# Layer 2: the first two products of the output projection start inside the attention

## The reference

```
def odd_mixer(h_lat, h_ctx, w_in, w_out, sink, cos, sin, ctx_out):
    q, k, v = odd_project(h_lat, w_in)
    ...
    y, yc = window_gqa_sink(q, k, v, qc, kc, vc, sink, ctx_out)
    return y @ w_out, ((yc @ w_out) if ctx_out else None)
...
        x_lat = layer_norm(DN_ALPHA * x_lat + m_lat[2] * y_lat, ln_g[l, 0], ln_b[l, 0])
        f_lat = conv_ffn(modulate(x_lat, m_lat[3], m_lat[4]), ffn_w_up[l], ffn_conv_w[l], ffn_conv_b[l], ffn_w_down[l])
        x_lat = layer_norm(DN_ALPHA * x_lat + m_lat[5] * f_lat, ln_g[l, 1], ln_b[l, 1])
```

## Time and profile before

| | |
|---|---|
| median of 3 runs | 2373.16 us |
| the profiled execution's own time | 2374.36 us |
| its span, first to last instruction | 2372.6 us |
| PE busy | 2282.4 us (96%) |
| DVE busy | 1564.1 us (66%) |
| ACT busy | 934.2 us (39%) |
| mean granted TensorE clock | 0.990 |

### The profile page before, as it was taken

How to read it: one execution, slowest core, us unless ns; L and a number is a source line. 1 busy time by engine, 2 the same in 40 slices (tenths; PEclk the granted TensorE clock), 3 DMA queues, 4 the chain that set the end, 5 groups by cost and what they waited for, 6 DMA issues and landing times.

```text
span 2372.6 us, 34992 instructions
## 1 busy us (share of the span) xinstructions
PE 2282.4 (96%) x14058; PEld 1868.4 (79%) x14058; DVE 1564.1 (66%) x2497; ACT 934.2 (39%) x1768; POOL 352.7 (15%) x455
## 2 busy tenths in 40 slices
PE   7999999999999899899999999999999999999998
PEld 3876667888887788777888888888887778888886
DVE  4548786566767652577779975656474877765457
ACT  5336553422222421576342332232352774424333
POOL 0110100011022210101010413213112120101131
PEclk9999999999999899999999999999999999999999
DMA  7430124644534312111322333324122112432321
GB/s 270 138 108 11 36 90 172 249 160 160 179 132 165 104 60 82 70 64 51 129 86 94 119 124 125 106 90 142 45 80 80 38 63 99 160 107 89 107 89 71
DMA packets 79473, 257.70 MB, mean 109 GB/s; under 512 B 5712, under 2 KB 10832, under 8 KB 70864
## 3 DMA queue, kind: packets, MB, share of 16 engines
q1 hardware_dynamic: 65888, 207.84, 25.4%
q0 software_dynamic: 12704, 46.14, 5.6%
q10 hardware_dynamic: 720, 1.47, 0.2%
HBM read 246.00 MB, written 9.44 MB: 108 GB/s over the span
## 4 chain that ended last, share of the span: by engine, by line
PE 48%; DVE 4%; ACT 2%; issue 1%; POOL 0%; POOLq 0%; DVEq 0%; ACTq 0%
PE PS L1310 8%; PE PS L1311 8%; PE PS L1312 8%; PE PS L1381 4%; PE PS L1382 4%; PE PS L1383 4%; PE PS L1182 1%; PE PS L1223 1%; PE PS L1279 1%; PE PS L1282 1%; PE PS L1280 1%; PE PS L1201 1%; PE PS L1016 1%; PE PS L1013 1%; PE PS L1014 1%
## 5 line engine op out<-in xcount | busy, mean ns | idle before, releaser
L1310 PE MATMUL PS<-HH,WH 128*128 128x512 f32 (+1 forms) x1088 | 420.4, 386 | 3.1 <-DVE WL L2401 1.7
L1311 PE MATMUL PS<-HL,WH 128*128 128x512 f32 (+1 forms) x1088 | 416.7, 383 | 0.0
L1312 PE MATMUL PS<-HH,WL 128*128 128x512 f32 (+1 forms) x1088 | 416.7, 383 | 0.0
L2811 ACT ACTIVATE WH<-STG 128x1024 fp32r<-128x1024 f32 (+1 forms) x202 | 196.9, 1023 | 270.1 <-PE PS L1383 222.2
L2401 DVE TENSOR_TENSOR WL<-STG,WH 128x1024 fp32r<-128x1024 f32 (+1 forms) x202 | 243.1, 1244 | 37.5 <-ACT WH L2811 37.3
L1923 DVE SCALAR_TENSOR_TENSOR ACC<-ADAW,CS,ACC 128x1024 f32<-128x1024 f32 x168 | 227.2, 1386 | 23.5 <-PE PS L1016 14.4
L1310 PEld LDWEIGHTS PS<-HH,WH 128*128 128x128 f32 x1088 | 204.4, 188 | 47.7 <-issue 6.2
L1312 PEld LDWEIGHTS PS<-HH,WL 128*128 128x128 f32 x1088 | 204.4, 188 | 40.4
L1311 PEld LDWEIGHTS PS<-HL,WH 128*128 128x128 f32 x1088 | 204.5, 188 | 40.0 <-issue 1.0
L1381 PE MATMUL PS<-WH,AH 128*128 128x512 f32 x600 | 234.9, 392 | 0.3 <-DVE AL L2629 0.3
L1382 PE MATMUL PS<-WL,AH 128*128 128x512 f32 x600 | 233.6, 389 | 0.0
(11 more groups left out here) (276 smaller groups left out, 4420.0 us busy)
## 6 DMA issues: line engine op xcount, KB each, us to landing
STG<-in_w_up SPq DMA_DIRECT2D x66, 1024.0 KB, 6.2
ADAW<-in_w_ada SPq DMA_DIRECT2D x96, 512.0 KB, 4.0
STG<-in_w_down SPq DMA_DIRECT2D x20, 1024.0 KB, 5.3
ADAW<-in_w_ada POOLq DMA_DIRECT2D x32, 512.0 KB, 4.1
STG<-in_w_ffn_out SPq DMA_DIRECT2D x10, 1024.0 KB, 7.3
STG<-in_ev_w_in SPq DMA_DIRECT2D x8, 1024.0 KB, 5.1
STG<-in_w_in SPq DMA_DIRECT2D x6, 1024.0 KB, 7.3
spill<-X POOLq DMA_DIRECT2D x10, 512.0 KB, 5.1
```

What stands on the lines that cost most here:

```text
L1310: e.matmul(out, h_, hh, start=c == 0, stop=False)
L1311: e.matmul(out, h_, hl, start=False, stop=False)
L1312: return e.matmul(out, l_, hh, start=False, stop=c == 7)
L2811: return e.activation(dst, src, ACT.Copy)
```

## The change

Only layer 2 is changed. Product (3,0) no longer stands in w_out: its first four chunks stand on PE behind the turning in turn 31 of the attention, its last four behind that in turn 32. Product (2,0) stands right behind the result of item 31, ahead of PE's wait for the other engines' ends. The other six products keep their order. So that this is possible, ACT makes the high parts of tile 3 in turn 30 and of tile 2 in turn 32, DVE the low parts of tile 3 in turn 31 and of tile 2 in turn 32; w_out keeps those of tile 4. The high part of tile 3 gets another place in REG, since at its old one lies the table of the window. The banks of the first two products are exchanged.

```
+def out_early(L):
+    return 2 if L == 2 else 0
@@ PE, woven_pairs
             if 1 <= i <= N:
                 turn(i - 1, 0)
+            if L == 2 and i in (N - 1, N):
+                out_product(2, 1, 0, range(4) if i < N else range(4, 8))
@@ PE, w_out
+        if L == 2:
+            out_product(2, 0, 0)
         for x in (k.dv_end, k.ac_end, k.pl_end):
             w.wait_ge(*x(("att", L)))
-        for i, n in out_order(L):
+        for i, n in out_order(L)[out_early(L):]:
+            out_product(L, i, n)
@@ PE, out_product (the loop body of before, in a function)
+        for c in cs:
+            wh, wl = k.out_weights(L, n, c // 4)
+            x = slice(c * P, (c + 1) * P)
+            w.wait_ge(*k.ac_xh((L, tt, c // 4)))
+            w.wait_ge(*k.dv_wolo((L, n, c // 4, c % 4 // 2)))
+            e.matmul(PS[:, b, :], xh[:, x], wh[:, c % 4, :], start=c == 0, stop=False)
+            e.matmul(PS[:, b, :], xh[:, x], wl[:, c % 4, :], start=False, stop=False)
+            w.wait_ge(*k.dv_xl((L, tt, c // 4)))
+            m = e.matmul(PS[:, b, :], xl[:, x], wh[:, c % 4, :], start=False, stop=c == 7)
@@ DVE, woven_pairs
                 inverse(i - 1)
+            if L == 2 and i == N - 1:
+                out_low(2, 1)
             if i >= 2:
                 result(i - 2)
             if 1 <= i <= N:
                 turned_p(i - 1, 0)
+            if L == 2 and i == N:
+                out_low(2, 0)
@@ ACT, woven_pairs
                 turned_p(i - 1, 0)
+            if L == 2 and i == N:
+                out_high(2, 0)
             if i < N:
                 powers(i, 1)
                 if L == 2:
                     sink(i)
+            if L == 2 and i == N - 2:
+                out_high(2, 1)
@@ DVE and ACT, w_out
-        for i in range(3):
-            low(i)
+        for i in range(out_early(L), 3):
+            out_low(L, i)
```

More of the change, by code:

```diff
@@ L370, in out_parts @@
         tt = WOUT_TT[L][i]
-        o = (10240, 11264, 0)[out_place(i)]
+        o = (10240, 12544 if L == 2 else 11264, 0)[out_place(i)]
         return self.split_att[L]["REG"][:, o:o + 1024], self.XL[:, tt * 1024:(tt + 1) * 1024]
@@ L1265, in pairs, with out_product @@
         a.close()
+    def out_product(L, i, n, cs=range(8)):
+        tt = WOUT_TT[L][i]
+        xh, xl = k.out_parts(L, i)
+        b = k.bank[("wo", L, tt, n)] if cs[0] else take(("wo", L, tt, n))
+        for c in cs:
[7 more added lines that the diff above has]
+            m = e.matmul(PS[:, b, :], xl[:, x], wh[:, c % 4, :], start=False, stop=c == 7)
+        if cs[-1] == 7:
+            m.then_inc(*k.pe_wout.up((L, tt) if n else (L, tt, 0)))
+            freed[b] = [k.dv_yg(("wo", L, tt, n))]
     def w_out(L, bg):
+        if L == 2:
+            out_product(2, 0, 0)
         for x in (k.dv_end, k.ac_end, k.pl_end):
             w.wait_ge(*x(("att", L)))
-        for i, n in out_order(L):
[L1271 to L1284, removed]
+        for i, n in out_order(L)[out_early(L):]:
+            out_product(L, i, n)
             if n:
@@ L1581, in tensor_program @@
         project(L)
-        rot["set"], rot["n"] = [6, 7], 0
+        rot["set"], rot["n"] = list(range(8)), 0
         scores_ready(L)
         woven_pairs(L, items_of(k, L))
-        rot["set"], rot["n"] = list(range(8)), 0
         e.drain().then_inc(*k.pe_end.up(("att", L)))
@@ L2237, in out_weights_low, with out_low @@
                         ALU.subtract).then_inc(*k.dv_wolo.up((L, n, h, i)))
+    def out_low(L, i):
+        xh, xl = k.out_parts(L, i)
+        tt = WOUT_TT[L][i]
+        for h in range(2):
+            x = slice(h * 512, h * 512 + 512)
+            w.wait_ge(*k.ac_xh((L, tt, h)))
+            e.tensor_tensor(xl[:, x], k.x(tt)[:, x], xh[:, x].bitcast(F32), ALU.subtract).then_inc(*k.dv_xl.up((L, tt, h)))
     def pairs(name, L, bg):
@@ L2410, in after @@
                 layer_norm("a", L, tt, [k.dv_x(("wo", L, tt, 1))])
[L2412 to L2418, removed]
         def regain(i):
@@ L2473, in w_out @@
             for x in out_made(L)[i]:
-                low(x)
+                out_low(L, x)
             if L and i != last - 1:
@@ L3032, in pairs, with out_high @@
         result(p)
+    def out_high(L, i):
+        xh, _ = k.out_parts(L, i)
+        tt = WOUT_TT[L][i]
+        if L == 2 and i < 2:
+            w.wait_ge(*k.dv_out((2, len(items_of(k, 2)) - 4 + (i + 1) % 2)))
+        if i >= 3:
+            w.wait_ge(*k.pe_wout((L, WOUT_TT[L][out_place_before(i)])))
+        for h in range(2):
+            x = slice(h * 512, h * 512 + 512)
+            copy(xh[:, x], k.x(tt)[:, x]).then_inc(*k.ac_xh.up((L, tt, h)))
     def woven_pairs(L):
@@ L3142, in norm @@
                 layer_norm("a", L, tt)
[L3144 to L3151, removed]
         for s in k.ends(("att", L)):
             w.wait_ge(*s)
-        for i in range(3):
-            high(i)
+        for i in range(out_early(L), 3):
+            out_high(L, i)
         for h in range(2):
@@ L3161, in w_out @@
             for x in out_made(L)[i]:
-                high(x)
+                out_high(L, x)
             if i == last:
```

## The result

The changed kernel takes 2378.61 us (median of 10 runs, 2377.67 to 2381.26), the kernel before in the same comparison 2373.14 us: +5.5 us, ratio 1.0023 with an interval of 1.0015 to 1.0031. The forecast was 2379.0. The profiled execution took 2378.48 us over a span of 2376.7.

The account below looks back on a forecast made before the run. PE bounds the feed-forward part, but a level chain of POOL's residual loads and DVE's work sets its start: 3.68 (later attention end) + 3.82 (SP's traffic) - 0.99 - 0.66 = +5.85 us, median 2379.0, range 2374.6 to 2380.8.

Parts of the forecast that it names:

- SP's fetch later: Feed-forward weight fetch, waiting for DVE's second piece of weights, goes from 1952.12 to 1953.55, only 1.43 us later.
- regain of tile 3 later: On DVE behind the residual loads: starts at 1968.1 instead of 1960.61, 7.5 us later; lower bound 3.68.
- DVE's waits for PE that go: DVE's waits of 0.99 and 0.66 us for PE's products vanish, since the products are done long before.
- The end of the attention: Two half products on PE, 2.72 us each, partly covering idle time, end the attention 3.68 us later; bounds 3.4 to 4.06.
- The early parts: ACT's and DVE's four early copies each hide in idle time and cost nothing; without that cover 0.5 us.
- PE's wait for weights: In w_out, PE needs the weights' second half at 1953.7 and gets it at 1952.4: no wait.
- The overtaking: SP's traffic keeps 3.4 us behind its issue and passes before tile 3 lands: 3.82 us more; forecast's chance 0.53.
- From the regain to the end: DVE's chain up to the second turn_mid: regain's 7.5 us less 1.65 of waits for PE gives 5.85 us later.
- The lost clock: Clock falls in PE's wait at turn_mid; 1.84 us lost in (5,0), covered to 0.2 us by 1.68 of later waits.
- No overtaking: Rival at the DMA queues: SP's traffic enters behind the same amount of POOL's; +2.0, 2375.2; chance 0.22.
- PE's gain: Rival at turn_mid: PE's 4.99 us come through if the POOL and DVE chain has room; 2368.3, chance 0.06.
- "worse" case: Rival: low clock pushes (5,1) and the first feed-forward product beyond DVE's chain; 2 to 3 us more, 2381.5; chance 0.05.

Follow-up runs that it names:

- e4: Changed kernel with product (3,0) in one piece behind the last result, ahead of (2,0), nothing inside the attention on PE: 2375.38 us, +2.6 against the kernel before.
- e1: Changed kernel with only (3,0)'s halves kept; product (2,0) and the parts of tile 2 back in w_out: 2376.93 us, +4.1 against the kernel before.
- e2: Changed kernel with only product (2,0) behind the last result; product (3,0) and tile 3's parts back in w_out: 2373.55 us, +0.7 against the kernel before.
- e3: Changed kernel with SP's first fetch of feed-forward weights held until tile 3's residual has landed: 2375.39 us, +2.6 against the kernel before.
- e6: Kernel before, with only SP's fetch held until tile 3's residual has landed: 2373.08 us, ratio 0.9998.
- e5: Edits of e2 and e3 together, one product behind the last result and SP's fetch held: 2370.63 us, -3.1 against the kernel before.
- e7: Kernel of e5 with POOL's two layer-norm gain loads issued behind the four residual tiles: 2370.70 us, -3.0 against the kernel before.
- e8: Changed kernel with SP's fetch held and the two gains loaded behind the residual tiles: 2371.06 us, -2.7 against the kernel before.

## Why the prediction was right

| step | predicted | measured |
|---|---|---|
| attention ends later | 3.68 | 4.17 |
| SP's fetch later | 1.43 | 1.94 |
| PE done with the products of tiles 2 to 4 earlier | 5.2 | 4.5 |
| more of SP's traffic ahead of tile 3 | 3.82 | 3.47 |
| regain of tile 3 later | 7.5 | 7.64 |
| DVE's waits for PE that go | 1.65 | both gone |
| second turn_mid later | 5.85 | 6.07 |
| time | +5.85 | +5.5 |

*The end of the attention.* The mechanism held, the term was 0.5 us too small, beyond the upper bound of 4.06 that I gave. The third matmul did not wait; what I left out are the borders between transposes and large matmuls: the row at 1942.39 is followed by the next matmul 0.34 us later and the last one, at 1945.02, by the inverse 0.32 us later, where I had 0.23, at four such borders, and a half starts 0.64 us behind its transposes, where I had 0.55. e4 against the changed kernel shows that the halves do it.

*The early parts.* I put them at nothing. In the changed kernel they are hidden; e4 shows 0.93 us where the half product doesn't cover them. I had put that price at 0.5.

*PE's wait for weights.* None, as predicted.

*The overtaking.* The mechanism held, the time came out so near by luck in part. I took SP's traffic to keep its 3.4 us behind the issue, with 1.88 MB of POOL's moved by then, 3.54 MB needed, and all of SP's 3.15 MB gone by before tile 3 lands, in either reading of the queues. None of this was exact. SP's first packet came 4.2 us behind the issue and its traffic in earnest 4.6 us, with 2.15 MB of POOL's moved; tile 3 needed 3.66 MB; POOL's queue had 0.159 MB/us beside SP's and not 0.145; and only 2.52 of SP's 3.15 MB had gone by. The later start and the higher need cost what the larger amount moved and the better rate give back, so the regain came at +7.64 against 7.5. The 3.82 us of the sum hide this: 1.11 MB more of SP's at 0.285 MB/us are 3.9 us, and 3.47 were measured.

Does SP's traffic start a fixed time behind its issue, or behind a fixed amount of POOL's? Five traces bear on it. Its first packet came 3.4 to 3.5 us behind the issue before, 4.2 in the changed kernel, 3.9 in e1 and e2, 4.2 in e4, with 2.8, 2.0, 2.3, 2.5 and 2.2 MB of POOL's moved in all. That speaks against the fixed 2.8 MB of the rival. Between issue and first packet POOL's moved 1.2 to 1.4 MB in all five; why SP's traffic waits so long stays open.

POOL's queue alone was slower than I thought, 0.25 MB/us from 1952 to 1955 against the 0.41 of the earlier trace rows, though all engines were busy; e3 shows that this stretch of its loads is slow without SP's traffic too (0.29). That the overtaking costs is shown by e3 (4.28 us less distance), by e6 (the regain 1.58 us earlier) and by the difference of e2 and e5 (2.5 us).

*From the regain to the end.* This step of the sum, the regain's shift less DVE's two waits for PE, is the best proved. In the changed kernel and in all eight experiments the distance is the shift of tile 3's regain, plus what DVE then waits for PE at the two places, less 1.65, within 0.16 us: 7.64 - 1.65 = 5.99 against 6.07 here, 3.39 - 1.65 = 1.74 against 1.79 in e3, -5.10 + 3.52 - 1.65 = -3.23 against -3.22 in e7.

*The lost clock.* As predicted, it costs nothing at the end: from (5,0) to the second turn_mid PE takes 18.78 us, 18.92 before, and its wait there fell from 1.31 to 0.16 us. The terms were off: the wait of 0.37 us ahead of the first feed-forward matmul stayed, so there was room for 1.31 us and not 1.68, and from (5,0) to that matmul PE lost 1.0 us (12.52 against 11.52) and not 1.84. A loss of 1.84 us would have gone 0.5 us beyond the room. The prediction names a rule by which transposes don't raise the clock, and the traces speak against it: see the last section.

*The rivals.* No overtaking (2375.2) is out: the regain would have moved by the 4.17 us of the attention's end, and it moved by 7.64. PE's gain didn't count in this kernel, and the profile said why: DVE's chain. e5 (-3.1) and e8 (-2.7) show that it does count, once SP's traffic stays behind the residual loads and, in the changed kernel, these stand ahead in POOL's queue too. The "worse" case did not come.

## What to carry to other kernels

Work put ahead of the instruction that ends a stage also puts off every transfer that waits for that end; find the last wait behind those transfers before counting the idle time that the work fills. Work put behind it is free of this price. And when the engines that prepare a stage get faster, look at which transfers they release: here a fetch that nobody read for 44 us (issued at 1952.08, first read at 1996.04) took the DMA engines from one that was needed at once. One wait on it made a nothing into a gain (e2, e5) and halved the loss of the changed kernel (e3); to make that loss a gain took an earlier place in the queue for the residual tiles as well (e8).

## What was not expected of the hardware

How much POOL's queue had moved when tile 3 landed differs: 3.54 MB before, 3.66 MB in the changed kernel, 4.04 MB in e3 without company, of 4.19 MB in all. Tile 3 is the sixth of eight loads of equal size, so it would be complete at 3.15 MB if they landed strictly one behind the other: they move partly together.

A group of 15 transposes took 3.74 us at 1.2 GHz, against 1.70 for 14 at 2.4 GHz.

The clock comes back while PE does nothing but transposes. In e3 it had fallen in the pause ahead of turn_mid (5.06 us); the 15 transposes start at 1979.47, product (5,0) at 1982.72, and in these windows (columns as above) it is back before the product:

```profile
1982.00:1982.50 0.50, 0.50 (x3) 0.53 0.00 0
1982.50:1983.00 0.50, 0.49 (x4) 1.00 0.00 0
```

That is 3.0 us into the transposes; in e1 and e4 it came back 2.8 and 3.0 us into them. Only in the changed kernel it lasted until 5.6 us behind their start, 2.2 us into the product.
